# A two-layer decoder trunk: opening transfers split, layer loop written out, two parameter loads and one multiply moved later

## The reference

```python
for l in range(2):
    z = rms_norm(x, mix_norm[l]) @ w_in[l]            # 1024 -> 4888 columns, split into parts
    o_a = sparse attention(z_q, z_kv, z_g, ..., cmp_pe, cmp_w1, cmp_w2)   # compressed, selected, window
    o_b = spatial_gating(z_sgu, ...)                  # u * (tril(W_s) v + b), 128-row chunks
    o_c = multiscale_pool(z_pool, ...)                # trailing means over 2, 4, 8, 16 rows
    x = x + (gated sum of o_a @ lift_a, o_b @ lift_b, o_c @ lift_c) @ w_out[l]
    x = x + memory attention(rms_norm(x), rms_norm(mem, mem_norm[l]), xa_wq, xa_wk, xa_wv, xa_wo)
    x = x + peer_ffn(rms_norm(x), ...)                # 16384 single-neuron experts, top 16 of 8 heads
```

## Time and profile before

| what | value |
|---|---|
| median of 3 runs | 2145.85 us |
| the profiled execution, its own time | 2146.53 us |
| its span in the profile | 2144.5 us |
| PE busy | 2120.7 us (99%) |
| POOL busy | 1716.0 us (80%) |
| DVE busy | 1239.9 us (58%) |
| ACT busy | 1191.5 us (56%) |
| granted clock of PE, mean | 1.00 |

### The profile page before, as it was taken

The page is one execution under the profiler, slowest core; times in us unless marked ns, Lnnn a source line. Parts: engine busy times, 40 slices in busy tenths (PEclk is TensorE's granted clock), DMA queues, the critical chain, the costliest instruction groups (busy, mean ns, idle before and its releaser), DMA issues.

```text
span 2144.5 us, 50206 instructions
## 1 busy us (share of the span) xinstructions
PE 2120.7 (99%) x14750; PEld 1839.9 (86%) x14750; DVE 1239.9 (58%) x2427; ACT 1191.5 (56%) x2289; POOL 1716.0 (80%) x1316
## 2 busy tenths in 40 slices
PE   7999999999999999999999999999999999999999
PEld 6878899999888888888878778999988888888887
DVE  5755458976666655433347564589666665553334
ACT  5555665555555545556555556655555555545565
POOL 6866778888878888888887576799888878888887
PEclk9999999999999999999999999999999999999999
DMA  7433445555454555565574334455544444556555
GB/s 273 161 133 118 156 145 168 185 176 176 167 167 159 169 172 166 186 200 189 189 247 152 123 130 140 150 183 180 180 169 168 168 166 161 172 168 199 192 186 176
DMA packets 100825, 367.98 MB, mean 172 GB/s; under 512 B 11520, under 2 KB 12160, under 8 KB 100480
## 3 DMA queue, kind: packets, MB, share of 16 engines
q1 hardware_dynamic: 97344, 354.46, 49.7%
q10 hardware_dynamic: 3392, 12.42, 1.6%
HBM read 365.78 MB, written 1.05 MB: 171 GB/s over the span
## 4 chain that ended last, share of the span: by engine, by line
PE 96%; issue 1%; POOL 1%; DVE 1%; ACT 0%; POOLq 0%; DVEq 0%
PE acc L1171 11%; PE acc L1257 11%; PE acc L1259 11%; PE acc L1258 11%; PE acc L1161 6%; PE acc L1162 6%; PE acc L1163 6%; PE acc L926 6%; PE acc L928 5%; PE acc L927 5%; PE acc L1170 5%; PE aux L1215 4%; PE aux L859 2%; POOL w_lo L471 1%; PE aux L1037 1%
## 5 line engine op out<-in xcount | busy, mean ns | idle before, releaser
L471 POOL TENSOR_TENSOR w_lo<-raw,w_hi 128x512 fp32r<-128x512 f32 x1312 | 1715.8, 1319 | 418.8 <-ACT w_hi L502 305.0
L502 ACT ACTIVATE w_hi<-raw 128x512 fp32r<-128x512 f32 x1348 | 843.9, 629 | 661.2 <-PE acc L928 175.4
L1257 PE MATMUL acc<-w_hi,eg 128*128 128x512 f32 x1024 | 402.6, 393 | 0.0
L1259 PE MATMUL acc<-w_hi,eg 128*128 128x512 f32 x1024 | 399.0, 390 | 0.0
L1258 PE MATMUL acc<-w_lo,eg 128*128 128x512 f32 x1024 | 398.5, 389 | 0.0
L1872 DVE TENSOR_TENSOR eg<-big,eg 128x256 fp32r<-128x256 f32 x256 | 170.0, 664 | 387.7 <-ACT eg L748 385.8
L1171 PE MATMUL acc<-h_rows,w_hi 128*128 128x512 f32 x1024 | 355.8, 397 | 0.0
L1161 PE MATMUL acc<-h_rows,w_hi 128*128 128x256 f32 x1024 | 290.4, 284 | 0.0
L1162 PE MATMUL acc<-h_rows,w_hi 128*128 128x256 f32 x1024 | 289.8, 283 | 0.0
L1163 PE MATMUL acc<-h_rows,w_lo 128*128 128x256 f32 x1024 | 289.8, 283 | 0.0
L1170 PE MATMUL acc<-h_rows,w_lo 128*128 128x256 f32 x896 | 249.7, 279 | 0.0
(11 more groups left out here) (266 smaller groups left out, 2977.0 us busy)
## 6 DMA issues: line engine op xcount, KB each, us to landing
raw<-stream_dram SPq DMA_DIRECT2D x674, 512.0 KB, 3.3
big<-parb_dram ACTq DMA_DIRECT2D x2, 2128.0 KB, 10.2
big<-mem_dram ACTq DMA_DIRECT2D x3, 1024.0 KB, 5.1
big<-pm_dram ACTq DMA_DIRECT2D x2, 768.0 KB, 14.8
X<-x_dram ACTq DMA_DIRECT2D x1, 1024.0 KB, 6.8
out_dram<-X SPq DMA_DIRECT2D x2, 512.0 KB, 3.0
big<-parr_dram ACTq DMA_DIRECT2D x2, 448.0 KB, 11.9
big<-lnrow_dram ACTq DMA_DIRECT2D x2, 256.0 KB, 13.0
```

What stands on the lines that cost most here:

```text
L471: nc.gpsimd.tensor_tensor(w_lo[:, k % SLOTS, :], raw[:, k // PER_CHUNK, k % PER_CHUNK, :], w_hi[:, k % SLOTS, :].bitcast(F32), ALU.subtrac ...
L502: nc.scalar.activation(w_hi[:, k % SLOTS, :], raw[:, (k // PER_CHUNK) % RAW, k % PER_CHUNK, :], ACT.Copy).then_inc(hi_ready, 1)
L1257: pe_.matmul(dst, eg[:, q % 2, 0, ts], w_hi[:, slot, :], start=start, stop=False)
L1259: ins = pe_.matmul(dst, eg[:, q % 2, 1, ts], w_hi[:, slot, :], start=False, stop=stop)
```

## The change

It does six things.

1. **Opening transfers.** The memory rows come in three transfers (columns 0 to 511, 512 to 767, 768 to 1023), the identity matrix and the other constants in one each. The first half and `col` count on a new semaphore `mem_first`, the identity on `ident_in`. `X` is issued by ACT behind its first weight piece. PE's first two groups of memory transposes wait for the first half only; DVE's waits for constants stand behind its memory rows.
2. **Early chunks.** SP issues chunk 0 with no wait, chunks 1 and 2 behind `mem_first`, chunk 3 behind the rest of the memory and the constants.
3. **Written-out layers.** On all four compute engines the hardware loop over the layers becomes a Python loop: each layer has its own copy of the instructions. `counts()` and `restart()` only keep Python's counters as they were.
4. **Parameters.** `pm` and `w1` are issued behind `hi_T("mix_T3")`, with `pm` first; the other four stay where they were.
5. **Wait and multiply.** DVE's wait for `params` and the multiply with `tril` stand behind `qk_mean`, just ahead of the adding of the table.
6. **Memory attention.** `lo_T("xo_T0")` stands ahead of the first `root_step`.

```diff
@@ sync
-            sp.wait_ge(sig["mem_in"].sem, 32)
-            sp.wait_ge(const_in, 16)
-            with sp.Fori(0, DEPTH * CHUNKS // RAW) as i:
+            for r in range(RAW):
+                if r == 1:
+                    sp.wait_ge(mem_first, 32)
+                if r == 3:
+                    sp.wait_ge(sig["mem_in"].sem, 32)
+                    sp.wait_ge(const_in, 16)
+                sp.dma_start(raw[:, r], stream[r:r + 1].rearrange("o p (k c) -> p (o k) c", c=COL)).then_inc(chunk_in[r], 16)
+            with sp.Fori(0, DEPTH * CHUNKS // RAW - 1) as i:
...
@@ gpsimd, scalar, tensor, vector (each)
-            with pool.Fori(0, DEPTH) as layer:
+            for layer in range(DEPTH):
...
@@ scalar
-            act.dma_start(memx, mem.rearrange("(t p) d -> p t d", p=P)).then_inc(sig["mem_in"].sem, 16)
-            act.dma_start(cst[:], consts).then_inc(const_in, 16)
-            act.dma_start(col[:], cols[0:1].rearrange("o p c -> p (o c)")).then_inc(sig["mem_in"].sem, 16)
-            act.dma_start(X[:], x.rearrange("(t p) d -> p t d", p=P)).then_inc(x_in, 16)
+            mem_rows = mem.rearrange("(t p) d -> p t d", p=P)
+            act.dma_start(memx[:, :, 0:COL], mem_rows[:, :, 0:COL]).then_inc(mem_first, 16)
+            act.dma_start(ident, consts[:, K_ID:K_ID + P]).then_inc(ident_in, 16)
+            act.dma_start(col[:], cols[0:1].rearrange("o p c -> p (o c)")).then_inc(mem_first, 16)
+            for at in (COL, COL + 256):
+                act.dma_start(memx[:, :, at:at + 256], mem_rows[:, :, at:at + 256]).then_inc(sig["mem_in"].sem, 16)
+            act.dma_start(cst[:, K_ID + P:K_END], consts[:, K_ID + P:K_END]).then_inc(const_in, 16)
...
             for i in range(4):
                 hi_piece(i, 16, i + 1)
+                if i == 0:
+                    act.dma_start(X[:], x.rearrange("(t p) d -> p t d", p=P)).then_inc(x_in, 16)
                 memory_hi(first, i)
...
-                for name, size, src in (("zgw", 256, zgw), ("w1", 4256, parb), ("sgw", 896, parr)):
-                    act.dma_start(...)
-                    hi(1)
-                act.dma_start(lnr, ...)
+                load_layer("zgw", 256, zgw)
                 hi(1)
-                act.dma_start(region("tril", 256), tril).then_inc(params, 16)
+                load_layer("sgw", 896, parr)
                 hi(1)
-                act.dma_start(big[:, OFF["pm"]:OFF["pm"] + 1536], pm).then_inc(params, 16)
+                load("lnrow", 512, ...)
                 hi(1)
+                load("tril", 256, tril)
+                hi(3)
...
                 hi_T("mix_T3", 6, 2, C_MIX + 6)
-                hi(4)
+                load("pm", 1536, pm)
+                hi(2)
+                load_layer("w1", 4256, parb)
+                hi(2)
@@ tensor
-            pe_.wait_ge(const_in, 16)
+            pe_.wait_ge(ident_in, 16)
+            pe_.wait_ge(mem_first, 32)
...
-                e.wait("mem_in")
+                if not start or i >= 2:
+                    e.wait("mem_in")
@@ vector
-            dve.wait_ge(const_in, 16)
...
-                d.wait("params")
-                d.step(V.tensor_tensor(sgw, sgw, trl..., ALU.mult), "sgw_ready")
...
                 mean(ssh, DK, "qk_mean")
+                d.wait("params")
+                d.step(V.tensor_tensor(sgw, sgw, trl..., ALU.mult), "sgw_ready")
...
+                lo_T("xo_T0", 0, 1)
                 root_step(xr[:, 4:8], xval, xtmp, ROOT_SCALE)
-                lo_T("xo_T0", 0, 1)
```

More of the change, by code:

```diff
@@ L349, in trunk @@
         x_in = sem("x_in")
+        ident_in, mem_first = sem("ident_in"), sem("mem_first")
         const_in = sem("const_in")
@@ L427, in forget, with counts, restart @@
                 s.sent -= count
+        def counts():
+            return [(s, s.sent) for s in list(sig.values()) + filled + drained]
+        def restart(layer, marks):
+            if layer < DEPTH - 1:
+                for s, n in marks:
+                    s.sent = n
         block = ctx.enter_context(nc.Block())
@@ L509, in _ @@
             forget(4, sig["mem_hi"])
-            with act.Fori(0, DEPTH) as layer:
+            for layer in range(DEPTH):
+                marks = counts()
                 a = Engine(act, layer, act_step)
@@ L570, in _, with load, load_layer @@
                 params = sig["params"].sem
[L571 to L575 removed]
+                def load(name, size, rows):
+                    act.dma_start(big[:, OFF[name]:OFF[name] + size], rows).then_inc(params, 16)
+                def load_layer(name, size, src):
+                    load(name, size, src[bass.ds(layer, 1)].rearrange("o p c -> p (o c)"))
+                load_layer("zgw", 256, zgw)
                 hi(1)
[L577 removed]
+                load_layer("sgw", 896, parr)
                 hi(1)
[L579 removed]
+                load("lnrow", 512, lnrow[bass.ds(layer, 1)].broadcast_to((P, 512)))
                 hi(1)
+                load("tril", 256, tril)
+                hi(3)
                 for i in range(2):
@@ L818, in _ @@
                 act.sem_clear(act_step)
+                restart(layer, marks)
         @block.tensor
@@ L823, in _, with memory_T @@
             pe_.sem_inc(used, SLOTS)
-            pe_.wait_ge(const_in, 16)
-            def memory_T(e, i):
-                e.wait("mem_in")
+            pe_.wait_ge(ident_in, 16)
+            pe_.wait_ge(mem_first, 32)
+            def memory_T(e, i, start=False):
+                if not start or i >= 2:
+                    e.wait("mem_in")
                 e.wait_bank_free(f"mem_T{i}")
@@ L838, in _ @@
             for i in range(4):
-                memory_T(first, i)
+                memory_T(first, i, True)
             forget(1, *filled)
-            with pe_.Fori(0, DEPTH) as layer:
+            pe_.wait_ge(const_in, 16)
+            for layer in range(DEPTH):
+                marks = counts()
                 e = Engine(pe_, layer)
@@ L1311, in _ @@
                 memory_lo(first, i)
+            dve.wait_ge(mem_first, 32)
             first.wait("mem_in")
@@ L1318, in _ @@
             dve.wait_ge(x_in, 16)
-            with dve.Fori(0, DEPTH) as layer:
+            dve.wait_ge(ident_in, 16)
+            dve.wait_ge(const_in, 16)
+            for layer in range(DEPTH):
+                marks = counts()
                 d = Engine(dve, layer, dve_step)
@@ L1423, in _ @@
                 mean(ssh, DK, "qk_mean")
+                d.wait("params")
+                d.step(V.tensor_tensor(sgw, sgw, trl.unsqueeze(1).broadcast_to((P, SGU_G, P)), ALU.mult), "sgw_ready")
                 for c in range(2):
```

8 lines of the change are left out of this document (2 added, 6 removed).

## The result

The changed kernel takes 2150.24 us (median of 20 runs, 2148.64 to 2152.45), the one before in the same runs 2146.08 (2145.66 to 2147.52): a ratio of 1.0018 with an interval of 1.0012 to 1.0025, or 4.2 us slower. The forecast was 2143.3 and its range ended at 2146.8. The profiled execution took 2150.3 us.

What follows compares the result with a forecast made beforehand. PE was taken as the bound, working 2120.7 of 2144.5 us, so only its waits could be won. Terms -2.8 - 0.9 - 0.2 + 1.6 - 0.3 = -2.6 gave 2143.9, as a median 2143.3 us; range 2139.3 to 2146.8.

Steps and rivals of the forecast that it cites:

- the sum: Whole kernel: the forecast's terms added, -2.8 - 0.9 - 0.2 + 1.6 - 0.3 = -2.6 us.
- the part's own other end: Late parameter loads: the forecast's bad end, one weight piece a layer missed, +2.8 us.
- rival C: Opening: X comes late and ACT stands at its squares, +3.7 for -2.8, sum +3.9; chance 0.08 with other losses.
- Rival B: Opening: chunk 1 lands slowly, so -2.8 becomes 0, sum +0.2, 2146.1 us; chance 0.12.
- Rival D: Between layers: PE didn't wait for the loop's jump, 0 for -0.9, 2144.2 us; chance 0.56 together with the forecast.
- Rival A: Key transposes: the late multiply stays covered, +1.6 falls away; with chunk 1 in time 2140.8 us; chance 0.24.
- theory D: Doubled late multiply: a PE wait of 2 us or more brings a lower-clock stretch, 1.6 us each, up to +8.3.

Runs made afterwards that it cites:

- e13: Changed kernel with the old opening back (opening transfers and early chunks undone), all else kept: 2151.40 us, ratio 1.0023.
- e2: Kernel before with only the new opening (split opening transfers, early chunks): 2144.78 us, ratio 0.9993.
- e14: Kernel before with written-out layers and the new opening (split transfers, early chunks): 2145.04 us, ratio 0.9994.
- e4: Kernel before with only the wait for params and the multiply moved behind qk_mean: 2148.27 us, ratio 1.0008.
- e6: Kernel before with the new opening, written-out layers and the lo_T swap in memory attention: 2145.86 us, ratio 0.9997.
- e1: Kernel before with only the layer loop written out on all four compute engines: 2144.91 us, ratio 0.9994.
- e9: Kernel before with the wait and multiply moved behind qk_mean and the multiply done twice there: 2149.68 us, ratio 1.0014.
- e7: Kernel before with written-out layers and pm and w1 issued late, the multiply in its old place: 2148.00 us, ratio 1.0009.
- e5: Changed kernel with the multiply back in its old place, the early four loads on their own semaphore: 2149.45 us, ratio 1.0013.
- e8: Changed kernel with w1's one transfer cut into four, issued in the same place: 2146.80 us, ratio 1.0001.
- e11: Changed kernel with w1 in four transfers and the multiply back in its old place: 2146.53 us, ratio 0.9997.
- e3: Kernel before with only pm and w1 issued late, the multiply in its old place: 2148.44 us, ratio 1.0009.

## Why the prediction was wrong, step by step

By the ledger the changed kernel is 4.05 us later at its end, in the profiled executions, where the sum had -2.6: 6.65 apart.

- **Part 4 failed, and most of all.** The step was "landing in up to 9.0 in place of 3.3 us, 5.7 later. The reserve is four slots of 1.4, 5.6 us: just enough. I take -0.2". Measured: +0.8 in layer 1 and +3.1 in layer 2, with the -0.2 that was said 4.1 of the 6.65, and more than the part's own other end, +2.8. The forecast had the right place and even the sign that would show it wrong (PE waiting for POOL between 42 and 60 us with ACT idle on a chunk: 0.98 at 55.48, behind 3.99 us of ACT). But it took 9.0, the longest landing in the kernel before, for the worst, and called a reserve enough that its own 5.7 already exceeds. The chunks behind `w1` landed in 9.4 and 10.4 us, because `w1`'s packets are four times as large as theirs; the forecast had counted bytes alone ("the same bytes move"). Of the 3.1 in layer 2 some 1.6 are the half clock behind the wait: e13 has the same wait, 2.02 us, without it, and pays 1.6. Cutting `w1` in four takes all of it away, in two kernels.
- **Parts 1 and 2: right up to the first matmul, mis-sized behind it.** First transpose 6.21 (said 6.1), first high rows 7.33 (7.15), `X` in time (it landed in 6.7 us, its squares at 16.16 against 18.56), so rival C is out (its own price was low as well: a third more than the 14.8 us of `pm` is 19.7, not 16). The step that failed is chunk 1: "I take 4.4: chunk 1 at 10.5". It was issued at 6.13, landed in 6.2 us, and its piece came at 12.42. That is 1.9 of the 2.2 us by which the part missed. Beside it went `X`, which ACT had issued at 4.64, not at 6.3, because chunk 0 had landed by then. "From there each step follows ACT's" was nearly right: DVE's squares start 0.95 earlier, as chunk 1's piece does, and the root 0.8; 0.2 went where DVE now meets POOL. -2.8 said, -0.6 at the row transposes in the changed kernel, -0.7 and -0.9 in e2 and e14: 2.2 of the 6.65. Rival B, that the opening gives nothing, was nearer than the forecast. PE's first matmul at 9.51 is followed by one gap of 0.57 and then full pace, the one at 12.91 by 0.59 and seven starts 0.43 apart, so even more had been won there and was given back in waits.
- **Part 3: the step itself right, its surroundings not.** Distance 0.60 (said 0.6), gap -0.9 (said -0.9). Rival D is out. "The jumps of ACT, POOL and DVE lie under work already prepared" was wrong: ACT's longer idle time at the jump (2.39 for 1.24 us) and its table load of 1.28 were paid by PE in layer 2's first rows; another -1.5 without them. Against it stand some +0.5 and +0.7 up to and in the memory attention of the two layers, in every kernel with written-out ACT, PE and DVE and in none of the others. Net about -1.2 in the changed kernel.
- **Part 5: right.** New waits for the keys of 0.95 and 0.86 us (said 0.5 to 1.3), 1.0 and 0.9 us in the ledger, 1.9 in e4, where it is alone; +1.6 said. Rival A is out.
- **Part 6: right as a mechanism, worth nothing.** The wait went from 1.39 to 0.66 (said 0.5); 272.42 then follows the stage's begin as before, +1.72 against +1.76 (e6 and e14, with and without the swap, lose alike there). -0.3 said, 0.0 measured.

The parts don't add. They move the instant at which DVE's operations start against POOL's pieces of 1.3 us, and by the rows above the same operation takes 0.17 or 1.29, 2.29 or 3.18, 3.60 or 5.54 us with it; by addition of e1 and e2 it would be -3.0 for the opening with written-out layers, and it is -1.3 in e14. That these meetings are the whole of the difference is argued; shown are the longer operations and the waits behind them.

## What to carry to other kernels

Where a transfer is moved beside a stream with a fixed reserve, compare the size of the two queues' packets and not only their bytes: with rows of 17 KB a partition beside 4 KB ones the stream got a fifth of the bytes and landed in up to 10.4 us against a reserve of 5.6, and cutting the big one in four at the same place took back 3.7 us. When writing out a loop, look at every engine's first instructions behind the jump, table loads among them: more was won there than in the gap itself. And when an opening is brought forward, follow each engine to the first point at which all of them meet (here the root at 24 us): only what arrives there is a gain.

## What the runs showed that was not expected

- **The granted clock of PE.** After PE's wait of 1.99 us at 1116.8 to 1118.8 in the changed kernel, eight matmuls come 0.43 us apart, half the pace, at the lower of the two levels (1.2 for 2.4 GHz; granted clock 0.50 from 1119.4 to 1122.7): 8 x 0.20 = 1.6 us. e13 waits 2.02 us in the same place and has no such stretch (1.00), and from 1094.6 to 1126 it pays 1.6 where the changed kernel pays 3.1. The changed kernel's own wait of 2.13 us at 27.5 has none behind it either, nor have e9's of 1.8 and e7's of 1.70 in layer 2, while e5's of 1.77 in layer 2 has one. So the length of the wait alone doesn't decide, against theory D. In e8, e5 and e11 a stretch lies at 28 to 32 us (granted clock 0.51), which is the +1.4 to +1.8 that they have at 32.3 against the changed kernel.
- **The steps in the runs.** The changed kernel's 20 runs lie in three groups, and the mean granted clock recorded with each run goes with them: five near 2148.8 (1.000 in four), eleven near 2150.2 (0.999 in ten), four near 2151.9 (0.998). So do those of e8 and e11: the four lowest of each (2145.2 to 2145.6, 2144.8 to 2145.1) have 1.000, the seven others 0.999 and are longer by 1.1 us or more. It looks as if runs had none, one or two such stretches; that is argued, since only one execution of each kernel has a trace. The five lowest runs of the changed kernel are 2.7 us above the kernel before, its median 4.2; the four lowest of e11 are 1.6 below it, its median level with it.
- **A clock that reads 1.00 at half pace.** The kernel before has matmuls 0.43 apart from 13.5 to 16.5 us, while the clock of that stretch reads 1.00; e1 has the same pace in the same place and reads 0.50. There the distance between starts is what counts.
- **An unbroken copy of the loop's code costs no more to fetch.** Twice the instructions on four engines, and no wait in layer 2 that only code loading explains.
- What stays open: what decides in a given run whether the lower clock follows a wait of 2 us; why the chunk behind `w1` lands after 10.4 us in layer 2 of the written-out kernels and after 9.4 in e3; and why the memory attention's exponential is 0.5 us late in all kernels with written-out ACT, PE and DVE (a small DVE operation ahead of it takes 1.25 in place of 0.17 us, one piece of POOL; it wasn't tried to move it).
